# Half of three output tiles done beside a triangular inversion, with float32r transposes, an earlier first input tile and rope angles, and later pooled parts

## The reference

```python
o_dn = gated_deltanet_group(dq, dk, dv, dz, db, da, ...)      # 4 heads of 128, chunked scan
o_at = axial_gqa_group(aq, ak, av, q_norm, k_norm)            # 8 heads of 64
mix = concatenate([o_dn, o_at], -1) @ w_out                    # 1024 x 1024
h = h + rms_norm(mix, norm_mix_post)
f = square(relu(rms_norm(h, norm_mlp_pre) @ w_up)) @ w_down
h = h + rms_norm(f, norm_mlp_post)
# inside the delta rule, for every chunk:
uw = triangular_solve(a_low + I, rhs)                          # unit lower triangular
v_new = u - w @ S;  o = q_dec @ S + qk @ v_new;  S = S * g_last + k_dec.T @ v_new
```

## Time and profile before

| | |
|---|---|
| median of 3 runs | 1471.34 us |
| lowest and highest | 1470.49 and 1472.98 us |
| the profiled execution | 1470.23 us |
| its span, first to last instruction | 1468.1 us |
| mean granted TensorE clock | 0.977 of 2.4 GHz |

### The profile page before, as it was taken

One profiled execution on the slowest core, in us unless ns is written; L12 is line 12 of the kernel. 1 busy time (PEld: TensorE's weight loads), 2 busy tenths in 40 slices (PEclk: granted clock), 3 DMA queues, 4 the chain that ended last, 5 costly groups with the idle time before them and its releaser, 6 DMA issues.

```text
span 1468.1 us, 19860 instructions
## 1 busy us (share of the span) xinstructions
PE 1373.4 (94%) x7309; PEld 1119.2 (76%) x7309; DVE 736.6 (50%) x1122; ACT 430.6 (29%) x838; POOL 768.2 (52%) x443
## 2 busy tenths in 40 slices
PE   7899999899999999999889999859989999999996
PEld 5777777677888887887878886638767888888885
DVE  6967766725545546114778885496534111211113
ACT  4254444413222122112344455333423111111111
POOL 5444533265666666674435432305254666676662
PEclk9999999999999999999999999978999999999998
DMA  5222212123233222222211111000031332222221
GB/s 192 92 81 72 87 59 70 44 89 111 89 100 100 96 90 100 94 92 86 72 59 44 58 44 58 15 1 2 15 101 58 100 100 100 88 99 100 98 88 58
DMA packets 31739, 113.85 MB, mean 78 GB/s; under 512 B 3520, under 2 KB 3904, under 8 KB 31424
## 3 DMA queue, kind: packets, MB, share of 16 engines
q1 hardware_dynamic: 31536, 112.85, 23.0%
q10 hardware_dynamic: 144, 0.18, 0.0%
HBM read 110.92 MB, written 2.10 MB: 77 GB/s over the span
## 4 chain that ended last, share of the span: by engine, by line
PE 83%; DVE 10%; ACT 4%; issue 2%; POOL 1%; DMA 1%; DVEq 0%; SPq 0%; ACTq 0%; POOLq 0%
PE ps L1038 41%; PE ps L1244 18%; PE ps L1382 6%; ACT arena L558 3%; PE ps L1057 3%; PE ps L1071 2%; PE ps L1264 1%; DVE arena L2077 1%; PE ps L1356 1%; PE ps L1186 1%; PE ps L1336 1%; PE ps L1175 1%; PE ps L1147 1%; DVE arena L2175 1%; DVE arena L2170 1%
## 5 line engine op out<-in xcount | busy, mean ns | idle before, releaser
L473 POOL TENSOR_TENSOR w_lo<-raw,w_hi 128x1024 fp32r<-128x1024 f32 x204 | 516.1, 2530 | 63.8 <-ACT w_hi L558 48.1
L468 POOL TENSOR_SCALAR w_hi<-raw 128x1024 fp32r<-128x1024 f32 x188 | 202.4, 1077 | 536.7 <-PE ps L1038 184.2
L1038 PE MATMUL ps<-h_hi,w_hi 128*128 128x512 f32 x944 | 376.4, 399 | 7.1 <-DVE arena L1687 4.3
L1038 PE MATMUL ps<-h_lo,w_hi 128*128 128x512 f32 x944 | 369.5, 391 | 0.0
L1038 PE MATMUL ps<-h_hi,w_lo 128*128 128x512 f32 x944 | 369.2, 391 | 0.0
L1038 PEld LDWEIGHTS ps<-h_hi,w_hi 128*128 128x128 f32 x944 | 178.2, 189 | 54.1 <-issue 10.4
L1038 PEld LDWEIGHTS ps<-h_lo,w_hi 128*128 128x128 f32 x944 | 178.1, 189 | 39.3 <-issue 2.9
L1038 PEld LDWEIGHTS ps<-h_hi,w_lo 128*128 128x128 f32 x944 | 178.3, 189 | 37.7
L558 ACT ACTIVATE arena<-ps 128x512 f32<-128x512 f32 (+6 forms) x201 | 96.4, 512 | 267.4 <-PE ps L1038 37.7
L558 ACT ACTIVATE arena<-arena 128x512 f32<-128x512 f32 (+6 forms) x191 | 101.4, 534 | 224.4 <-DVE arena L2323 134.2
L1244 PE MATMUL ps<-g_hi,w_hi 128*128 128x512 f32 x400 | 155.7, 389 | 0.9 <-DVE arena L1933 0.9
(11 more groups left out here) (284 smaller groups left out, 1834.3 us busy)
## 6 DMA issues: line engine op xcount, KB each, us to landing
raw<-in_w_stream SPq DMA_DIRECT2D x204, 512.0 KB, 3.4
xT<-in_x_t SPq DMA_DIRECT2D x2, 1056.0 KB, 7.1
out<-xT SPq DMA_DIRECT2D x8, 256.0 KB, 2.1
C<-in_cst SPq DMA_DIRECT2D x1, 576.0 KB, 10.1
arena<-in_cst SPq DMA_DIRECT2D x1, 528.0 KB, 4.3
arena<-in_pos SPq DMA_DIRECT2D x1, 256.0 KB, 4.0
V<-in_vec ACTq DMA_DIRECT2D x1, 174.5 KB, 5.8
band<-in_cst SPq DMA_DIRECT2D x1, 160.5 KB, 3.7
```

The costliest lines, as they stand in the source:

```text
L468: pool.tensor_scalar(w_hi[j][:], raw[j % 2][:], 1.0, 1.0, ALU.mult, ALU.mult).then_inc(S["pool_step"], 1)
L473: pool.tensor_tensor(w_lo[j][:], raw[j % 2][:], w_hi[j][:], ALU.subtract).then_inc(split_done[j], 1)
L1038: last = mm(dst[p], w[:, k, :], h[:, k, cols], start=(k == 0 and n == 0), stop=(k == KT - 1 and n == 2))
```

## The change

1. **Start.** x tile 0 gets a transfer of its own ahead of unit 0; tiles 1 to 3 and 4 to 7 are issued behind unit 0. POOL rounds `w_hi[0]` in two halves, and TensorE starts its first tile on the first half. ACT does tile 0 as soon as it and `V` are there.
2. **DVE order.** The constant copies `masks` (the identity in float32r among them), the reciprocal of the counts and the first five instructions of `rope_angles` move ahead of the wait for `rs_ready`. The rest of `rope_angles` follows `windows(0)`. `window_parts(0)` moves behind `qk(0)`, `window_parts(1)` behind `qk(7)`.
3. **Gate before side.** `gate(0)` runs before `qk_side(8)`.
4. **Transposes.** All TensorE transposes read data and identity as float32r.
5. **Attention half early.** For output tiles 2 and 3 (k = 4 to 7) and 1 (k = 4 to 6), `w_hi` and `w_lo` read as float32 are multiplied with `AQ` in float32, beside the inversion: 22 matmuls. Tiles 2 and 3 stay in banks 7 and 3; tile 1 is copied by ACT to SBUF (`spill`) and added by DVE at the end.
6. **Levels.** ACT copies the first direction's diagonal blocks (4 instructions); banks are renumbered.
7. **Scan.** `state` and its key product are left out in the last step, whose result nothing reads. POOL does `queries(0)` after the first key products.
8. **Output.** Every tile has a bank of its own. Tile 1 is read from `spill` plus bank. The last tile is copied first and squared second, like the others.

```diff
@@ SP, POOL and TensorE at the start
-            sp.dma_start(xT[:, 0:4, :], x_t[:, 0:4, :]).then_inc(S["x_loaded0"], 16)
+            sp.dma_start(xT[:, 0:1, :], x_t[:, 0:1, :]).then_inc(S["x_first"], 16)
...
                         if j == 0:
+                            sp.dma_start(xT[:, 1:4, :], x_t[:, 1:4, :]).then_inc(S["x_loaded0"], 16)
                             sp.dma_start(xT[:, 4:8, :], x_t[:, 4:8, :]).then_inc(S["x_loaded1"], 16)
...
+                            k0 = 4
+                            pool.tensor_scalar(w_hi[0][:, 0:4, :], raw[0][:, 0:4, :], 1.0, 1.0, ALU.mult, ALU.mult).then_inc(S["w_first"], 1)
+                        pool.tensor_scalar(w_hi[j][:, k0:KT, :], raw[j % 2][:, k0:KT, :], 1.0, 1.0, ALU.mult, ALU.mult).then_inc(S["pool_step"], 1)
@@ DVE
+            dve.wait_ge(S["c_loaded"], 16)
+            for n, name in enumerate(("ident", "neg_f", "neg_b")):
+                last = v.tensor_copy(masks[:, n, :], cst_ap(name))
+            last.then_inc(S["masks_ready"], 1)
+            dve.wait_ge(S["misc_loaded"], 32)
+            step(v.reciprocal(cnt16, cnt16))
...
+            step(v.tensor_copy(posf, posi))
...
             dve.wait_ge(S["rs_ready"], 1)
...
                 windows(g)
-                if g < 2:
-                    window_parts(g)
-                if g == 1:
+                if g == 0:
                     rope_angles()
...
                     last_window(t - 2)
+                if t in (1, 8):
+                    window_parts(t // 8)
@@ TensorE
+            def turned_into(dst, src):
+                return nc.tensor.transpose(dst.bitcast(F32R), src, masks[:, 0, :])
...
-            qk_side(8)
...
             gate(0)
+            qk_side(8)
...
+            def early(f, ks):
+                u = (U_OUT2 + f) % 4
+                pe.wait_ge(split_done[u], rounds(U_OUT2 + f))
+                for k in ks:
+                    mm(out2_bank(f), w_hi[u][:, k, :].bitcast(F32), AQ[:, k - 4, :], start=(k == 4), stop=False)
+                    last = mm(out2_bank(f), w_lo[u][:, k, :].bitcast(F32), AQ[:, k - 4, :], start=False, stop=(k == 6 and f == 1))
+                return last
+
             pe.wait_ge(S["b_act"], 9)
+            early(2, range(4, 8))
             pe.wait_ge(S["meta_dve"], 3)
...
+            pe.wait_ge(S["b_act"], 12)
+            early(3, range(4, 6))
...
-            pe.wait_ge(S["b_act"], 12)
+            early(3, range(6, 8))
+            early(1, range(4, 7)).then_inc(S["early_done"], 1)
             pe.wait_ge(S["lev_dve"], lev_dve("BE"))
@@ scan, TensorE
-                state(st, 0)
+                if st < 3:
+                    state(st, 0)
                 v_new(st, 1)
                 output(st, 0)
-                state(st, 1)
+                if st < 3:
+                    state(st, 1)
@@ output projection, TensorE
-            tile_pair(U_OUT2, 4, [[ps[:, 0, :]], [ps[:, 1, :]]], order=(4, 5, 6, 7, 0, 1, 2, 3),
-                      ready=lambda k: (S["att_ready"], k - 3) if k >= 4 else (S["h_ready"], parts_before(4) + k + 1))
-            for f in range(1, KT):
-                if f > 1:
-                    wait(pe, S["sq_ready"], 24 + f - 1)
-                    tile(U_OUT2 + f, 0, [ps[:, f % 2, :]])
+            for k in range(4, 8):
+                pe.wait_ge(S["att_ready"], k - 3)
+                out2_part(0, k, k == 4, False)
+            out2_part(1, 7, True, False)
+            for k in range(4):
+                pe.wait_ge(S["h_ready"], parts_before(4) + k + 1)
+                for f in range(2):
+                    last = out2_part(f, k, False, k == 3)
+                    if k == 3:
+                        last.then_inc(unit_done[f], 1)
+            for f in range(2, 4):
+                for k in range(4):
+                    last = out2_part(f, k, False, k == 3)
+                last.then_inc(unit_done[f], 1)
+            for f in range(4, KT):
+                tile(U_OUT2 + f, 0, [out2_bank(f)])
```

More of the change, by code:

```diff
@@ L276, in build @@
         KD_m = [ST[1][d][0:META] for d in range(2)]
+        spill = C[:, P:P + T]
         od1 = OD.rearrange("p a b -> p (a b)")
@@ L531, in _ @@
             pool.wait_ge(S["b_act"], 12)
-            queries(0)
             pool.wait_ge(S["lev_pe"], lev_pe("X5", 1))
             pool.wait_ge(S["lev_dve"], lev_dve("Y"))
-            for st in range(NB):
+            pool.wait_ge(S["diag_y"], 4)
+            for st in range(NB - 1):
                 for d in range(2):
@@ L541, in _ @@
                                        ).then_inc(kdt_ready[d], 1)
-                if st < 3:
-                    queries(st + 1)
+                if st == 0:
+                    queries(0)
+                queries(st + 1)
             n = U_OUT2 // 4 + 1
@@ L921, in _ @@
                 act.wait_ge(S["meta_done"], d + 3)
-                a(VN_m[d], ps[0:META, 4 + d, :].rearrange("p (a b) -> p a b", b=P), ACT.Copy).then_inc(S["meta_act"], 1)
+                a(VN_m[d], ps[0:META, 4 + 2 * d, :].rearrange("p (a b) -> p a b", b=P), ACT.Copy).then_inc(S["meta_act"], 1)
+            act.wait_ge(S["early_done"], 1)
+            a(spill, out2_bank(1), ACT.Copy).then_inc(S["spill_done"], 1)
             for g, q0 in LEVELS:
@@ L1310, in _ @@
                 c0 = META + P * b if b < 4 else 0
-                last = nc.tensor.transpose(ps[:, 6 + b // 4, (b % 4) * P:(b % 4) * P + P], x5[:, 1, c0:c0 + P], cst_ap("ident"))
+                last = turned_into(ps[:, 6 + b // 4, (b % 4) * P:(b % 4) * P + P], x5_r[:, 1, c0:c0 + P])
             last.then_inc(S["v2_turned"], 1)
@@ L1459, in _ @@
             for h in range(4):
-                nc.tensor.transpose(ps[:, 1, h * P:(h + 1) * P], DK[:, h, 0:P], cst_ap("ident"))
-                last = nc.tensor.transpose(ps[:, 2, h * P:(h + 1) * P], DV[:, h, 0:P], cst_ap("ident"))
+                turned_into(ps[:, 1, h * P:(h + 1) * P], DK_r[:, h, 0:P])
+                last = turned_into(ps[:, 2, h * P:(h + 1) * P], DV_r[:, h, 0:P])
             last.then_inc(S["meta_done"], 1)
@@ L1958, in _ @@
             m_low(M1, 0, 1, 5)
-            for n, name in enumerate(("ident", "neg_f", "neg_b")):
-                last = v.tensor_copy(masks[:, n, :], cst_ap(name))
-            last.then_inc(S["masks_ready"], 1)
             dve.wait_ge(S["ba_loaded"], 16)
@@ L2297, in add_normed @@
                 v.tensor_tensor(xT[:, f, REAL], xT[:, f, REAL], src[:, f, :], ALU.add).then_inc(S["x_ready"], 1)
+            product(dve, U_OUT2 + 1)
+            dve.wait_ge(S["spill_done"], 1)
+            v.tensor_tensor(mixb[:, 1, :], out2_bank(1), spill, ALU.add).then_inc(S["spill_added"], 1)
             for f in range(KT):
```

113 lines of the change are left out of this document (67 added, 46 removed).

## The result

The kernel after takes 1459.16 us (median of four runs, 1458.83 to 1462.09); in the same comparison the kernel before took 1471.93 us. The ratio is 0.9919, with a 95% interval of 0.9905 to 0.9934. So the change gains 12 to 13 us (11.9 by the ratio, 12.8 by the medians) of the 25.3 that were predicted, and the time lies above the range of 1436 to 1456. The profiled execution took 1459.13 us, its span 1457.3, against 1468.1 before.

A forecast was written before the change was run, and what follows sets the result against it. TensorE's own work was taken to set 83% of the end, DVE's 10%. Terms 0.5 + 7.0 + 1.5 + 6.6 + 1.3 + 1.4 + 7.0 = 25.3 us, from 1471.34 to 1446.0 us; range 1436 to 1456.

The forecast's parts named there:

- Start: First transfers and roundings: the eighth `h_lo` comes earlier, gaining 0.5 us, bounds 0 and 1.5.
- Input stage: TensorE's wait for DVE at 58 us and the half clock after it go: 7.0 us gained, bounds 5 and 7.5.
- DVE is still late: Rival: more long DVE instructions lose half of the input stage's 7.0 and the 1.5 us; 1450.3 us, chance 6%.
- Behind the last q tile: TensorE's 2.1 us wait for ACT goes, but `pooled(0)` then needs `window_parts(1)`: 1.5 us gained, bounds 0.4 and 2.3.
- Without it, at the same moment: Without DVE's 2.76 us instruction in `qk(7)`, `window_parts(1)` would be done just when TensorE is ready; with it, 1.9 us later.
- Transposes: Both attentions: float32r transposes at 0.083 us instead of 0.110, 244 of them; 6.6 us gained, bounds 0 and 12.9.
- I count 244: Of the two attentions' 272 transposes, 244 stand where TensorE sets the pace, so cheaper ones gain time.
- the rivals of 0.110 and 0.057: Transposes stay at 0.110 us each: 1452.6 us, chance 25%; or fall to 0.057: 1439.7 us, chance 15%.
- if the clock holds: Condition in the levels: half of TensorE's 5.12 us at clock 0.50 goes only if full clock lasts.
- Early half: Beside the inversion: 22 float32 matmuls and meta products take 22.5 of 22.4 us; levels start 0.1 to 0.3 us late.
- Levels: Inversion's levels: 1.5 us gained from full clock, less 0.2 for the late start: 1.3 us, bounds -0.5 and 2.5.
- Scan and output projection: Two `state` pieces leave the scan, 1.4 us gained; 33 matmuls leave the output projection, 7.0 us gained, bounds 5.5 and 7.5.

## Why the prediction was wrong

The direction and the mechanisms of most steps were right; four terms were too large, and the clock, which costs time of its own, stood in none. Of the 14.2 us that are missing 3.4 are in the input stage, 1.4 behind the last q tile, 2.1 in the transposes, 3.9 are the new half clock and 3.6 are in the inversion and levels; the last term had 0.2 more.

- **Start, 0.5.** Found 0.5 to 0.9.
- **Input stage, 7.0.** The step that failed is "the moved work fits into DVE's 5.15 us of idle time ... 3.6 in all", and with it "at least 8.2 us, so `pool_in(4)` is there at about 54". I priced DVE's instructions by their short form. Beside GpSimd's subtractions (2.4 to 2.7 us each) DVE's own instructions stand, and the moved ones were put right beside them: 7.5 us in place of 3.6. `pool_in(0)` came 1.1 us later than before (36.26 for 35.14), `pool_in(2)` 3.7 us later (49.03 for 45.33). The wait and the half clock at 58 did go, as predicted; 2.8 us came back as the two waits, for `pool_in(0)` and `pool_in(2)`. With the subtraction cut the stage gains the predicted 7.5 us in full (7.7), but the cut also frees what stood in the kernel before, so how much of it the move would give by itself is not shown. The row that showed it was quoted as the earlier trace rows, and my rival "DVE is still late" named it, at 6% and at half the price; I hadn't asked what made 0.7 into 2.76.
- **Behind the last q tile, 1.5.** Found 0.1. "Without it, at the same moment" was the mistake again: two instructions of 2.7 to 2.8 us stand in that list (lines 1850 and 1848), and the run with `window_parts(1)` earlier showed that DVE's list as a whole, with what GpSimd adds to it, is what `pooled(0)` waits for.
- **Transposes, 6.6.** The price was right: 0.081 us for the 0.083 taken, and the rivals of 0.110 and 0.057 are excluded. By the Trainium skill's rule on loading ("TensorE: Matmul & The Clock Gate", section on LDWEIGHTS) 128 columns take an estimated 107 ns. Taken as the least distance between transposes, as the prediction took it, this doesn't hold for the float32r ones; the measurement decides. The count was wrong: "I count 244". In the second attention about 63 of 160 count (1.9 us / 0.030), since every second group has a wait for ACT behind it that grows by what the group saves; in the first about 87 of 112 (2.6 us / 0.030). Together 4.5 us.
- **Clock.** No term of the sum had it, though "if the clock holds" stands beside the levels. In the profiled execution three new stretches cost 3.9 us. One of them, at 275, comes with the float32r transposes in every profile. The other two are not in every profile. Beside the k and v blocks a fourth (954.4 to 957.8) costs 1.5 us more; it stands in the term of the levels.
- **Early half.** "The levels start 0.1 to 0.3 us late": they start 1.8 us late. The work is near its price: 963.68 to 986.8, 23.1 us where I counted 22.5. The larger error was the room. I took the 22.4 us of the trace before; in the profiled execution it is 21.3, 963.68 to DVE's end at 984.98. The half clock from 954.4 to 957.8, beside the k and v blocks, made it so: with the same program and the half clock ahead of those blocks it is 22.8, and the levels start 0.3 us late, as predicted. So the step holds in one kind of execution and fails in the other, and a margin of zero can't hold that.
- **Levels, 1.3.** Found -2.3 in these two profiles: 1.6 us more of a late start; the clock was again at half from 991.9 to 998.8, so the gain of 1.5 did not come; and 0.5 for ACT's copies, which I had called beside the chain. The run without them says 0.8 to 1.5.
- **Scan and output projection, 1.4 + 7.0.** Found 8.6. Right in size, though the terms written down for the projection sum to 6.8 and I took 7.0; no run takes the scan's edit or the banks alone.

Still open is why the clock falls at 275 to 282 with the cheaper transposes: TensorE is as little busy there in the kernel with float32 ones. What comes before differs only in how long the transposes take, and I didn't try anything that would separate the two.

## What to carry to other kernels

A duration in a profile belongs to its neighbour too: before moving DVE work, look at what GpSimd does at the new place, and take a row that is four times its sisters as a question, not as a scatter. A gap on one engine ends when the other side is done; here the same program had 21.3 or 22.8 us of room by where half clock fell, so a fit to within a few tenths is no fit. Work moved to an engine with idle time is only free if nothing that the chain needs stands behind it on that engine's list.

## What the runs showed of the hardware

- An instruction of 32 columns on DVE (0.19 us) took 2.27 or 2.31 us when it started while GpSimd subtracted, so size gave no protection. Which instructions are hit changes from run to run: with the same list ahead of it `pool_in(0)` came at 36.1 to 36.4 in some kernels (two hit; 37.1 with edit 1 undone) and at 38.3 to 38.6 in others (three hit), at 36.26 and 38.62 with one and the same program.
- The same holds where neither kernel was changed. Seven additions of DVE with two SBUF inputs, ahead of the norm's root, take 13.47 us (13.44 in the kernel before), where one that nothing holds takes 0.68. All but the first last 1.35 or 2.70 us, in turn, beside GpSimd's roundings (1.36 to 1.5 us) and subtractions (2.65); the run above cut no subtraction there:

```profile
14.98 13.47 DVE L1744 TENSOR_TENSOR arena<-arena 128x512 f32<-128x512 f32 x7
```

- Eight float32r transposes of 128x128 in a row take 0.65 us, 0.081 each, eight float32 ones 0.89, 0.111 each.
- The stretch at half clock from 60 to 67 is gone, but others came: the profiled kernel after has 48 us at half clock between 16 us and 1440, the kernel before 58. Beside the inversion and the levels it has 7 where that one has 27, so elsewhere it has 10 us more.
